# Two weight units per token tile at the start, unmasked window blocks alone, gate norm between drains, earlier taps and a merge product in halves

## The reference

```python
h = rms_norm(x, ln1_g); z_a, z_b, z_c, z_g = split(h @ w_in)
u, v = split(gelu(z_a)); v = layer_norm(v)
y_a = (u * chunked_spatial_gating(v)) @ w_a_out
p, g = split(z_b); c = p * sigmoid(g)
c = silu(layer_norm(causal_depthwise_conv(c, 31 taps)))
y_b = c @ w_b_out
y_c = stick_breaking_attention(rms(q), rms(k), v) @ w_c_out
x = x + (sig(z_g0) * y_a + sig(z_g1) * y_b + sig(z_g2) * y_c) @ w_out
x = x + ffn(rms_norm(x))                      # w_up, 3-tap conv, w_down
# second block
u, g_rnn, q, k, v, g_attn, m_r, m_a = split(rms_norm(x) @ w_in_2)
y_rnn = rg_lru(conv4(u)) * silu(g_rnn)
y_attn = sliding_window_attention_with_sinks(rope(q), rope(k), v) * silu(g_attn)
x = x + (sig(m_r) * y_rnn @ w_rnn_out + sig(m_a) * y_attn @ w_attn_out) @ w_o
out = rms_norm(x, final_norm_g)
```

## Time and profile before

| | us |
|---|---|
| runs of the kernel before | 1323.57, 1326.31, 1326.85 (median 1326.31) |
| profiled execution | 1323.74 |
| its span, first to last instruction | 1321.8 |
| TensorE busy | 1298.2 |
| VectorE busy | 844.5 |
| ScalarE busy | 609.5 |
| mean granted clock of TensorE | 0.996 of full |

### The profile page before, as it was taken

How to read it: one execution, slowest core, us unless ns; L and a number is a source line. 1 busy time by engine, 2 the same in 40 slices (tenths; PEclk the granted TensorE clock), 3 DMA queues, 4 the chain that set the end, 5 groups by cost and what they waited for, 6 DMA issues and landing times.

```text
span 1321.8 us, 15645 instructions
## 1 busy us (share of the span) xinstructions
PE 1298.2 (98%) x5991; PEld 1046.0 (79%) x5991; DVE 844.5 (64%) x1110; ACT 609.5 (46%) x886; POOL 85.6 (6%) x70
## 2 busy tenths in 40 slices
PE   7999999999999999999999999999999999999997
PEld 6887777788777888888888888887877777778886
DVE  5458789889976776666665335435368878445534
ACT  6234467232263443333343224423389999544232
POOL 0000222000000200000000002100012220000000
PEclk9999999999999999999999999999999999999999
DMA  7432111422322322222222222422312221214211
GB/s 235 184 103 68 64 64 65 155 75 89 97 94 76 116 96 95 95 95 95 95 95 96 95 95 94 162 96 96 96 64 87 73 80 65 96 64 159 96 64 64
DMA packets 98282, 128.73 MB, mean 97 GB/s; under 512 B 2952, under 2 KB 80688, under 8 KB 97712
## 3 DMA queue, kind: packets, MB, share of 16 engines
q1 hardware_dynamic: 98208, 127.93, 28.7%
q10 hardware_dynamic: 16, 0.00, 0.0%
HBM read 121.63 MB, written 6.29 MB: 97 GB/s over the span
## 4 chain that ended last, share of the span: by engine, by line
PE 90%; DVE 7%; ACT 2%; DMA 1%; issue 1%; SPq 0%; DVEq 0%; ACTq 0%
PE PS L1683 87%; PE PS L1750 3%; DVE WL L1030 1%; ACT WH L585 1%; DMA STAGE<-in_w_in 1%; DVE QK L1132 0%; DVE CACC L1184 0%; DVE XL L1066 0%; DVE XG L1058 0%; DMA LNR<-in_ln_g 0%; DVE VSG L1160 0%; DVE MERG L1294 0%; DVE MERG L1355 0%; DVE MERG L1369 0%; DVE TMPY L1352 0%
## 5 line engine op out<-in xcount | busy, mean ns | idle before, releaser
L585 ACT ACTIVATE WH<-STAGE 128x1024 fp32r<-128x1024 f32 x214 | 225.8, 1057 | 489.5 <-PE PS L1683 473.6
L1030 DVE TENSOR_TENSOR WL<-STAGE,WH 128x1024 fp32r<-128x1024 f32 x214 | 276.3, 1293 | 228.3 <-ACT WH L585 227.8
L1683 PE MATMUL PS<-XH,WH 128*128 128x512 f32 x960 | 383.5, 399 | 2.4 <-DVE CPAD L1239 2.4
L1683 PE MATMUL PS<-XH,WL 128*128 128x512 f32 x960 | 375.6, 391 | 0.0
L1683 PE MATMUL PS<-XL,WH 128*128 128x512 f32 x960 | 375.4, 391 | 0.0
L1683 PEld LDWEIGHTS PS<-XH,WH 128*128 128x128 f32 x960 | 181.1, 189 | 45.1 <-issue 4.6
L1683 PEld LDWEIGHTS PS<-XL,WH 128*128 128x128 f32 x960 | 181.3, 189 | 38.7 <-issue 2.4
L1683 PEld LDWEIGHTS PS<-XH,WL 128*128 128x128 f32 x960 | 181.0, 189 | 38.3
L1683 PE MATMUL PS<-WH,XH 128*128 128x512 f32 x224 | 88.3, 394 | 1.1 <-DVE XL L1066 1.1
L1683 PE MATMUL PS<-WL,XH 128*128 128x512 f32 x224 | 87.3, 390 | 0.0
L1683 PE MATMUL PS<-WH,XL 128*128 128x512 f32 x224 | 87.3, 390 | 0.0
(11 more groups left out here) (298 smaller groups left out, 1840.1 us busy)
## 6 DMA issues: line engine op xcount, KB each, us to landing
STAGE<-in_w_in SPq DMA_DIRECT2D x52, 1024.0 KB, 4.9
STAGE<-in_w_up SPq DMA_DIRECT2D x22, 1024.0 KB, 5.0
STAGE<-in_w_down SPq DMA_DIRECT2D x11, 1024.0 KB, 4.8
STAGE<-in_w_out SPq DMA_DIRECT2D x4, 1024.0 KB, 4.8
STAGE<-in_w_rnn_out SPq DMA_DIRECT2D x4, 1024.0 KB, 4.9
STAGE<-in_w_attn_out SPq DMA_DIRECT2D x4, 1024.0 KB, 4.7
STAGE<-in_w_o SPq DMA_DIRECT2D x4, 1024.0 KB, 4.9
XTOK<-in_x SPq DMA_DIRECT2D x4, 512.0 KB, 6.1
```

The source lines that it names most:

```text
L585: act.activation(ring(WH, n), staged(n), ACT.Copy).then_inc(hi_done, 1)
L1030: dve.tensor_tensor(ring(WL, n), staged(n), ring(WH, n).bitcast(F32), ALU.subtract)\
L1683: return pe.matmul(out_, lhsT, rhs, start=start, stop=stop, skip_group_check=True)
```

## The change

Seven edits:

1. SP issues token tile 0, weight transfer 0, then token tiles 1 to 3. TensorE runs units 0 and 1 together over token tile 0, then tile 1, and so on (first_units). ScalarE and VectorE make the parts of units 0 and 1 earlier.
2. Score, mask, maximum, exponential, transpose, copy and scale of the 4 windows of the first query block cover 128 keys instead of 256.
3. The first two drains of U_B stand ahead of and between the gate norm's tiles.
4. The taps are dealt out 4 instead of 3 from i = 6 on and 4, 4, 4, 4, 6, 3 in the groups of six units, so none is left behind the last group; mean, squares and root each stand one unit sooner.
5. Unit U_C + 33 signals each of its four output tiles, and VectorE multiplies each when it is there. lo(U_D + 1) stands behind these merges.
6. The first two units of w_out run k = 0 to 3 both, then k = 4 to 7 both.
7. At the end the left 512 columns are multiplied by the gain early (VectorE) and by the root's reciprocal on ScalarE, the right 512 on VectorE; each half is stored by a transfer of its own.

The diff, cut to its core (left out are the buffer and semaphore declarations, the mask's construction, counts of constants, and lines that only take the same two arguments again):

```diff
@@ -127,6 +127,11 @@
     return (((0, 0), (1, 128)), ((2, 0),), ((3, 0),))[s % 3]
+
+
+def first_key(w):
+
+    return 0 if w % TT else P
@@ -426,12 +432,11 @@
-            for t in range(2):
-                sp.dma_start(XTOK[:, t, :], xt[:, t, :]).then_inc(x_in[t], 16)
+            sp.dma_start(XTOK[:, 0, :], xt[:, 0, :]).then_inc(x_in[0], 16)
             for p, src in enumerate(transfers()):
                 kd, ncol = src.shape[1], src.shape[2]
                 if p == 1:
-                    for t in range(2, TT):
+                    for t in range(1, TT):
                         sp.dma_start(XTOK[:, t, :], xt[:, t, :]).then_inc(x_in[t], 16)
@@ -474,10 +479,12 @@
             for t in range(TT):
+                ot = out.rearrange("o (t p) d -> p (o t) d", p=P)
+                sp.wait_ge(fin_left, t + 1)
+                sp.dma_start(ot[:, t, 0:512], XT2[:, t, 0:512]).then_inc(stored, 16)
                 sp.wait_ge(fin_ready, t + 1)
-                sp.dma_start(out.rearrange("o (t p) d -> p (o t) d", p=P)[:, t, :], XT2[:, t, :])\
-                  .then_inc(stored, 16)
-            sp.wait_ge(stored, 16 * TT)
+                sp.dma_start(ot[:, t, 512:1024], XT2[:, t, 512:1024]).then_inc(stored, 16)
+            sp.wait_ge(stored, 32 * TT)
@@ -612,12 +617,12 @@
+            hi(0)
             x_high(0)
             x_copy(0)
-            hi(0)
+            hi(1)
             x_high(1)
             x_copy(1)
-            hi(1)
             x_high(2)
@@ -860,7 +865,7 @@
                         j = 2 * par + idx
-                        act.activation(buf[:, par, idx, :], buf[:, par, idx, :], ACT.Exp,
+                        act.activation(buf[:, par, idx, first_key(w):], buf[:, par, idx, first_key(w):], ACT.Exp,
                                        bias=SMALL[:, c0 + 4 + j:c0 + 5 + j],
@@ -1011,6 +1017,10 @@
                                        SMALL[:, S_FIN + t:S_FIN + t + 1], ACT.Sqrt).then_inc(fin_sd, 1)
+                        act.wait_ge(fin_rcp, t + 1)
+                        act.wait_ge(fin_gain, t + 1)
+                        act.activation(XT2[:, t, 0:512], XT2[:, t, 0:512], ACT.Copy,
+                                       scale=SMALL[:, S_FIN + t:S_FIN + t + 1]).then_inc(fin_left, 1)
@@ -1072,14 +1082,14 @@
             x_gain(0)
+            lo(0)
+            x_low(0)
             x_gain(1)
-            x_low(0)
-            lo(0)
+            lo(1)
             x_low(1)
             x_gain(2)
             x_gain(3)
             x_low(2)
-            lo(1)
             x_low(3)
@@ -1162,9 +1173,9 @@
             taps_done = 0
-            tap_order = [(c, j) for j in range(12) for c in (0, 1)]
-            tap_order += [(c, j + (12 if c < 2 else 0)) for j in range(CVK - 12) for c in range(KW)]
-            tap_order += [(c, j) for j in range(CVK - 12, CVK) for c in (2, 3)]
+            tap_order = [(c, j) for j in range(15) for c in (0, 1)]
+            tap_order += [(c, j + (15 if c < 2 else 0)) for j in range(CVK - 15) for c in range(KW)]
+            tap_order += [(c, j) for j in range(CVK - 15, CVK) for c in (2, 3)]
             tap_place = {cj: place for place, cj in enumerate(tap_order)}
@@ -1237,6 +1248,12 @@
                 dve.tensor_tensor(dst, PS[:, i % 2, :], RBC[:], ALU.mult).then_inc(drained, 1)
+                if i < 2:
+                    gate_norm(2 * i)
+                if i == 1:
+                    pair_mask(0)
+                if i < 2:
+                    gate_norm(2 * i + 1)
                 if i == 1:
@@ -1256,7 +1273,7 @@
                 if i >= 4:
-                    taps(3)
+                    taps(3 if i < 6 else 4)
                 if 1 <= i < 13:
@@ -1298,10 +1315,12 @@
                                .then_inc(bl_ready, 1)
-                        taps(4)
-
+                        taps((4, 4, 4, 4, 6, 3)[r])
+
+            assert taps_done == KW * CVK
             for p in range(10):
-                dve.wait_ge(unit_done, U_C + 24 + p + 1)
+                if p < 9:
+                    dve.wait_ge(unit_done, U_C + 24 + p + 1)
                 if p < 8:
@@ -1310,28 +1329,26 @@
                        .then_inc(drained, 1)
-                lo(U_C + 24 + p + 4)
+                if p < 9:
+                    lo(U_C + 24 + p + 4)
                 if p == 0:
-                    taps(4)
-                    assert taps_done == KW * CVK
-                if p == 1:
                     dve.wait_ge(c_tap, KW * CVK)
                     link(dve.tensor_tensor(TG1[:], CACC[:, 0, :], CACC[:, 1, :], ALU.add))
                     link(dve.tensor_tensor(TG0[:], CACC[:, 2, :], CACC[:, 3, :], ALU.add))
                     dve.tensor_tensor(TG1[:], TG1[:], TG0[:], ALU.add).then_inc(c_sum, 1)
-                if p == 2:
+                if p == 1:
                     dve.wait_ge(c_mean, 1)
                     for c in range(KW):
                         dve.scalar_tensor_tensor(CACC[:, c, :], PS[:, 4, :], -1.0 / W, CACC[:, c, :],
                                                  ALU.mult, ALU.add).then_inc(c_cent, 1)
-                if p == 3:
+                if p == 2:
                     dve.wait_ge(c_sq, 2)
                     link(dve.tensor_tensor(TG0[:], UU[:, 0, :], UU[:, 1, :], ALU.add))
                     dve.wait_ge(c_sq, 3)
                     link(dve.tensor_tensor(TG0[:], TG0[:], UU[:, 2, :], ALU.add))
                     dve.wait_ge(c_sq, 4)
                     dve.tensor_tensor(TG0[:], TG0[:], UU[:, 3, :], ALU.add).then_inc(c_ssum, 1)
-                if p == 4:
+                if p == 3:
                     dve.wait_ge(c_var, 1)
@@ -1354,12 +1375,13 @@
                            .then_inc(merged, 1)
+            lo(U_D + 1)
             for m in range(4):
                 merged_low(m)
             for m in range(4):
                 if m < 3:
-                    dve.wait_ge(quad_done, m + 1)
+                    dve.wait_ge(quad_done, 3 + m + 1)
                 else:
@@ -1664,6 +1687,10 @@
             for t in range(TT):
+                dve.wait_ge(fin_sq, t + 1)
+                v = XT2[:, t, 0:512]
+                dve.tensor_tensor(v, v, FG[:, 0:512], ALU.mult).then_inc(fin_gain, 1)
+            for t in range(TT):
                 dve.wait_ge(out_done, t + 1)
@@ -1672,8 +1699,9 @@
                 dve.wait_ge(fin_sd, t + 1)
-                link(dve.reciprocal(s_, s_))
-                dve.scalar_tensor_tensor(XT2[:, t, :], XT2[:, t, :], s_, FG[:], ALU.mult, ALU.mult)\
+                dve.reciprocal(s_, s_).then_inc(fin_rcp, 1)
+                dve.wait_ge(fin_rcp, t + 1)
+                dve.scalar_tensor_tensor(v, v, s_, FG[:, 512:1024], ALU.mult, ALU.mult)\
                    .then_inc(fin_ready, 1)
@@ -1767,6 +1795,22 @@
+            def first_units(t):
+                first_tile(t)
+                ts = slice(t * P, (t + 1) * P)
+                for n in (U_A, U_A + 1):
+                    if t == 0:
+                        unit(n)
+                    for k in range(2):
+                        kk = 2 * (n - U_A) + k
+                        last = split_mm(PS[:, t, :], XH[:, kk, ts], XL[:, kk, ts],
+                                        ring(WH, n)[:, k, :], ring(WL, n)[:, k, :], kk == 0, False)
+                    if t == TT - 1:
+                        last.then_inc(unit_done, 1)
+
+            for t in range(TT):
+                first_units(t)
+
             for j in range(4):
@@ -1901,19 +1947,26 @@
                     cm_unit(U_C + 24 + p, p % 4, XH, XL)
-                    if p == 2:
+                    if p == 1:
                         pe.wait_ge(c_sum, 1)
                         pe.wait_ge(drained, DR_C + 32)
                         mm(PS[:, 4, :], ONES[:], TG1[:], True, True).then_inc(c_mean, 1)
-                    if p == 4:
+                    if p == 3:
                         pe.wait_ge(c_ssum, 1)
                         mm(PS[:, 5, :], ONES[:], TG0[:], True, True).then_inc(c_var, 1)
                 pe.wait_ge(c_cent, KW)
                 pe.wait_ge(c_ve, 1)
                 pe.wait_ge(bh_ready, 3)
                 pe.wait_ge(bl_ready, 3)
-                for u in range(2):
-                    quad_unit(U_C + 32 + u, u, 4, BH, BL, KW)
+                quad_unit(U_C + 32, 0, 4, BH, BL, KW)
+                n = U_C + 33
+                unit(n)
+                for m in range(4):
+                    for k in range(2):
+                        last = split_mm(PS[:, 4 + m, :], ring(WH, n)[:, k, m * P:(m + 1) * P],
+                                        ring(WL, n)[:, k, m * P:(m + 1) * P], BH[:, 2 + k, :],
+                                        BL[:, 2 + k, :], False, k == 1)
+                    last.then_inc(quad_done if m < 3 else unit_done, 1)
                 pe.wait_ge(drained, DR_C + 40)
@@ -1935,14 +1988,23 @@
-            for m in range(KD):
+            for h in range(2):
+                for m in range(2):
+                    if h == 0:
```

(25 more changed lines are left out.)

64 lines of the change are left out of this document (36 added, 28 removed).

## The result

The changed kernel takes 1308.4 us (median of four runs, 1308.0 to 1309.3) against 1324.9 us; the ratio is 0.9875, with a 95% interval of 0.9862 to 0.9889. The forecast was 1308.5. The profiled execution took 1308.09 us with a span of 1306.27 us, 15.6 us less than the 1321.84 us of the span before. TensorE's busy time fell by 9.2 us, the other 6.4 us are waits. The kernels of the experiments ran in other sets of runs than the changed kernel, and the kernel before has medians from 1323.5 to 1325.5 us in those sets.

A forecast was written before the change was run, and what follows sets the result against it. TensorE was taken as the bound, busy 1298.2 of 1321.8 us; terms 1.1 + 4.1 + 3.2 + 3.5 + 3.3 + 0.7 + 0.5 = 16.4 us gave 1307.3 to 1309.9, forecast 1308.5, range 1304 to 1312.5.

The forecast's parts named there:

- Start: First units over the token tiles: two waits for XL go, first matmul some 0.5 us later; net 1.1 us gained.
- A: Letter for the term Start, two units per token tile: 1.1 us gained, between 1.5 lost and 2.0 gained.
- the rule on transposes: Skill's statement that transposes don't count as clock activity, so the start stays cold until matmuls; the forecast held the trace against it.
- Gate norm: Drains of U_B ahead of and between the norm's tiles: TensorE's drain wait, restart and half clock go; 4.1 us gained.
- Taps: Taps two units sooner: six moved into the attention stretch at no cost, the sum let go earlier; 3.2 us gained.
- C: Letter for the gain at the sum: a wait of 1.3 to 1.4 us replaces 2.8, half clock goes; 3.2 us.
- Rival 2: Attention stretch: VectorE about a microsecond late at each last step, six holes costing 3 to 9 us; 1312 to 1317, chance 0.10.
- Rival 3: Attention stretch: POOL's product holds up all 24 taps, 19 us of holes plus half clock; 1336 us, chance 0.02.
- Merge's product: Merges made quarter by quarter ahead of the output product: three waits for MH go; 3.5 us gained, 2.5 at least.
- D: Letter for the term Merge's product, ahead of the output product: 3.5 us gained.
- Masked blocks: Four of 16 windows with halved score matmuls and fewer transposes: 3.3 us, plus 0.7 at the first window's gate.
- End: Behind the last matmul: last product halved over two engines, two stores; 0.5 us gained, between 0 and 0.9.

The follow-up runs named there:

- no_merge: The changed kernel with the merge's product made as before (one signal for its whole unit, each output unit over all eight k at once); 1313.83 us.
- only_start: The kernel before with the changed start alone (first weight transfer ahead of token tile 1, two units per tile); 1322.29 us against 1324.46.
- only_gate: The kernel before with the gate norm and the mask of step 0 put between the drains, alone; 1320.37 us against 1323.49.
- only_mean: The kernel before with the new counts of taps and the sum's steps one unit sooner, alone; 1323.24 us, ratio 0.9991.
- poolhalves: The changed kernel with GpSimd's product of a step in two instructions, one for each half, instead of one; 1307.46 us.
- v2: The changed kernel with the mask ahead of the WL step, eight more transposes at the start, only the last tile halved and one store a tile; 1305.16 us.
- onestore: The changed kernel with the last product still in two halves, but one store of 1024 columns a token tile instead of two of 512; 1308.76 us.
- v3: The kernel v2 with the three sums of the convolution's output moved behind the last taps; 1303.69 us, ratio 0.9837.

## Why the forecast was right, point by point

The time was right to 0.1 us, but not each term: the misses of 1.4, -1.9 and -0.8 us in the start, the attention stretch and the end mostly cancel, and 0.5 us more in the others helps. That is luck. So is part of the last step: the sum of 16.4 us, taken from the profile, gave 1307.3, and from the median of three runs 1309.9; a fourth run put that median at 1324.9, from which it gives 1308.5.

**Start (1.1 forecast, 2.46 here): mis-sized.** Tile 1 landed at 8.44 as forecast (8.5), the waits for XL went (1.6 us with restarts). The step that failed is "the 24 transposes, 0.215 us each, then run from 8.5 to 13.7". They ran in 4.40 us, since the clock rose while they ran. In most relatives it rose later, the first matmul came at 13.4 to 13.8, near the forecast, and A was worth about 1.5 us, 0.9 in no_merge; over ten runs of only_start it was 2.2. The weighing of the rule on transposes went the right way, but was then not carried through to the pace of the transposes themselves. (Its ground was thinner than it said: in the trace of before the first 128x512 matmul is still slow, 0.57 us to the next, so the clock rose while that one ran.)

**Gate norm (4.1): right**, 4.12 in this trace and 4.1 at this place in only_gate's; that kernel's median gain is 3.1 us, since it loses 0.6 later on and other holes stay open. What only the runs showed is that 1.6 of it are the clock's, and that part isn't certain: in only_mean the same hole had no stretch of half clock behind it.

**Taps (C 3.2, and nothing for the attention stretch): right and wrong.** The sum's wait is 1.25 us (1.3 to 1.4 forecast), the half clock is gone, 3.17 us. The step that failed is "VectorE is busy 50.5 of 57.8 us: 4.1 of 7.3 us of slack, so I cost them at nothing". By the forecast's own sign ("Wrong if a wait for BT or GB sigmoids shows") this term was wrong. Part of that slack was the time in which GpSimd's product ran while VectorE waited for WH. With a fourth tap the scan ends later, the product starts later, VectorE no longer waits but is held up by it, and the chain scan, product, WL step, mask has nothing between its links. Rival 2 named the place and, at 3 to 9 us, overstated the price: two holes of 0.96 and 0.72 us came, not six. And the sentence on the Trainium skill, SBUF — State Buffer, SBUF: two separate sides, said that the rule "would leave the sum as it is". The Trainium skill says there that the one which starts first has the shared port for its whole instruction, and this holds here (poolhalves shows the lock for one instruction, in both directions). By it the one operation that waits is the WL step, which stands ahead of the mask; followed one step further it would have moved the sum: the WL steps take 2.5 to 2.8 us where they took 1.2 to 2.3. Rival 3 didn't come: in the steps the taps stayed at 0.68 us each. Its price was misread, too. The two taps in 3.54 us at 220.25 are not 1.77 each: the records give 0.73 us for the first, which starts ahead of GpSimd's product, and 2.90 us for the second, which starts behind it. One operation waits, and no other.

**Merge's product (3.5): right**, 3.71, and no wait for MH. But D can be worth more: no_merge's median is 5.4 us above the changed kernel's. Of the 6.6 us between the two profiles 3.5 are the waits, 1.5 a clock that fell behind them, and 1.6 the start, which has nothing to do with D. The profile of before showed these waits with no half clock behind them, and the forecast took that for a property of short holes.

**Masked blocks (3.3 and 0.7): right**, 0.8 to 0.9 us for each of three windows and 1.7 for the first with its gate.

**End (0.5): wrong sign.** The halves do gain what was forecast: 6.14 us from the last add to the end in v2 against 6.63 before. A fetch of instructions inside the last store, which no row of before could show, takes 0.66 of it back (6.80 in onestore). The changed kernel's other 0.1 us can't be told from the spread of the traces.

**From the profile to the median.** The forecast went between 1307.3 and 1309.9 on the ground that the slower runs of before may hold further half-clock stretches. The runs fit that: over 13 runs of the kernel before the time goes from 1322.6 us at a mean clock of 0.997 to 1327.0 at 0.993, while the changed kernel's four have 0.998 to 0.999 and v3's five lie within 0.4 us. The profiles give 15.6 us, the medians 16.5.
